# Hyena taps in pairs from both row halves, two of them ahead of the stage barrier, in a hybrid trunk kernel

## The chip, the cores and the metric

One core of one Trainium2 chip. The metric is the device time of one execution in microseconds, the median over the runs; lower is better.

## What is computed

One layer of a trunk runs over 512 latent tokens and 128 context tokens: a normalised, modulated input goes through four parallel head groups (gated DeltaNet, HGRN2, mLSTM, Hyena), their outputs are joined and projected by w_out, and a mixture of 64 experts with top 8 follows. The change touches the Hyena group's filters and, beside them, the last steps of HGRN2. Cut to what matters:

```python
def _hyena_filters(length, w1, b1, w2, b2, w3, freq):
    ...
    hid = jnp.sin(freq * (feats @ w1 + b1))
    hid = jnp.sin(freq * (hid @ w2 + b2))
    h = (hid @ w3).reshape(length, HYENA_ORDER, 2, W_D)
    ...
    h = h * jnp.exp(-tn[:, None] * deltas[None, :])[:, None, None, :]
    circ = jnp.concatenate([h[:, :, 0], zero, h[:0:-1, :, 1]], axis=0)
    circ = circ * lax.rsqrt(jnp.sum(circ * circ, axis=0, keepdims=True) + EPS)
    return jnp.fft.rfft(circ, axis=0)

def longconv(z, o):
    zf = jnp.fft.rfft(z, n=2 * l, axis=1)
    return jnp.fft.irfft(zf * hf[None, :, o], n=2 * l, axis=1)[:, :l] + dbias[o] * z

z = x1 * longconv(v, 0)
return x2 * longconv(z, 1)
```

The product hid @ w3, times the decay, gives the taps: one filter of length 512 for the latent tokens and one of length 128 for the context, five tiles of 128 lags in all.

## The kernel before, in words

All engines run programs written out by hand, with semaphores between them. SBUF is one tensor "arena", PSUM one tensor PS of eight banks of 512 f32 columns for 128 partitions. There are two stages with an all-engine barrier between them: the first (blocks from L505, TensorE's program from L619) holds the projections and the heads of the three recurrent groups, the second (from L2305, TensorE's from L2392) the Hyena group, w_out, the router, the experts and the final norm. At the seam all engines meet (end of the block, L505), meet again (L2181), GpSimd clears the stage's semaphores, and they meet a third time (L2184).

**End of the first stage.** HGRN2 goes through HU units of 128 tokens. Each has LV levels (hgrn_level, L1142 to L1154, written alternately for the two row halves of the array: partitions 0 to 63 and 64 to 127 hold two heads), whose results lie in banks 4 and 5 or 6 and 7 and are merged by DVE (L1661), then hgrn_out (L1168, L1171) in bank 2. After the last unit TensorE waits for n_on and n_taken (the last gate_heads of DVE, L1686 and L1687, which reads banks 0 and 1), transposes tiles 1 to 4 of the HGRN heads for pt 0 and 1 (L1222), and then tile 0 (L1227, behind n_last). For pt 0 the transposes go to bank 0 (tiles 1 to 3) and bank 1 (tile 4), for pt 1 to banks 4 and 5. DVE multiplies them into yT (L1737, L1738, L1742); its last step ends the stage. hid2 (the hidden layer of the filter net: 64 rows for lag tiles 0, 1, 2 and the other 64 rows for tiles 2, 3, 4) and w3sd (sum and difference of w3's sides, present in both row halves) have been in SBUF since the projections and since unit 2.

**Start of the second stage.** TensorE's order is written out at the end of its Hyena functions: filter_taps(0) to (4), forward(0, 0), forward(0, 1), filter_spectrum(0), filter_spectrum(1), prompt_spectrum, filter_norms, gate rows, and the inverse transforms. filter_taps (L2406 to L2412) makes a tile t: two matmuls (side 0 and 1) of 64 rows, 128 by 512, into banks 4 and 5 for even t and 6 and 7 for odd t; tiles 0 to 2 use rows 0 to 63, tiles 3 and 4 rows 64 to 127. A tile from the third on waits until DVE has taken the one two before it. An f32 matmul leaves two records in the trace. forward(0, j) (L2457 to L2464) is the signal's transform: 8 matmuls of 128 by 256 in banks 2j and 2j+1. filter_spectrum (L2428 to L2441) is 8 matmuls of 128 by 512 for each j (two small ones more for j = 0, L2440) in banks 4 to 7, then 0 to 3; the first waits for all five tiles (f_hs 5) and f_lag 1, the second for c_sd 2.

DVE multiplies each tile by the decay into hsd (L2723, f_hs), then takes the signal's sums and differences (L2742, L2746, L2747: c_sd), then tables(0) (L2733), a few one-row steps (L2754 to L2759: f_row), tables(1), and products (L2783 on). ACT squares each tile (L3057, f_sq) and copies the signal's odd part (L3068: c_odd) in the order: squares 0 to 3, odd part 0, square 4, odd part 1, then odd_out (L3061), table copies (L3072). POOL halves the lag-0 row of tile 0 (first_lag, L3183 and L3185: f_lag), adds the squares of tiles 1, 2, 3 to that of tile 0 (L3193: f_sum; each waits for its square, and ACT's next square waits for the sum before), then halves the row of tile 4 and makes gate_diag (L3200). SP loads the inverse's and the context's transform matrices at the start of the stage (L2310, L2311) and w_out later, behind f_H 3.

Of the kernel before, what the change touches and what calls it, by code (L numbers as in the profile page):

```python
# [17 lines left out]
P = 128  # L18
# [106 lines left out]
def trunk_program(nc, T):  # L125
# [14 lines left out]
    with ctx:  # L140
# [359 lines left out]
        filt_in, siren_step = sem("filt_in"), sem("siren_step")  # L500
        SIREN = dict(layer1=1, phase1=2, hidden1=3, layer2=4, phase2=5, hidden2=6)
# [3 lines left out]
        with nc.Block() as block:  # L505
# [113 lines left out]
            def _(pe):  # L619
# [581 lines left out]
                for u in range(HU):  # L1201
# [12 lines left out]
                    if u < NO_STATE:  # L1214
                        hgrn_state(u)
                pe.wait_ge(n_on, 3)
                pe.wait_ge(n_taken, 4)
                for pt in range(2):
                    b = 4 * pt
                    for t in range(1, NT):  # L1220
                        dst = PS[:, b, t * P:(t + 1) * P] if t < 4 else PS[:, b + 1, 0:P]
                        mm = pe.transpose(dst, o_tok[:, 1, t, P * pt:P * pt + P], ident)  # L1222
                    mm.then_inc(n_tr, 1)
# [8 lines left out]
            def _(dve):  # L1232
# [500 lines left out]
                for pt in range(2):  # L1733
                    dve.wait_ge(n_tr, 5 + pt)
                    y, b = yT[:, 2 + pt, :], 4 * pt
                    dst, src = by_column(y)[:, 16:, :], PS[:, b, P:SMP].rearrange("p (w r) -> p w r", r=SMP // GW)
                    dve.tensor_tensor(dst, dst, src, ALU.mult)  # L1737
                    dve.tensor_tensor(y[:, SMP:TOK], y[:, SMP:TOK], PS[:, b + 1, 0:P], ALU.mult)  # L1738
# [566 lines left out]
        with nc.Block() as block:  # L2305
# [86 lines left out]
            def _(pe):  # L2392
# [12 lines left out]
                def filter_taps(t):  # L2405
                    if t >= 2:  # L2406
                        pe.wait_ge(f_hs, t - 1)
                    r, a = (slice(0, HD), t * P) if t < 3 else (slice(HD, P), (t - 2) * P)
                    for side in range(2):
                        mm = pe.matmul(PS[:, 4 + 2 * (t % 2) + side, :], hid2[r, a:a + P],  # L2410
                                       w3sd[r, side].rearrange("p o n -> p (o n)"), start=True, stop=True)
                    mm.then_inc(f_h, 1)  # L2412
# [106 lines left out]
                for t in range(NT):  # L2519
                    filter_taps(t)  # L2520
                forward(0, 0)
                forward(0, 1)
                filter_spectrum(0)
# [193 lines left out]
            def _(dve):  # L2717
                dve_order = Steps(dve, "dve_order2")
                MAGIC = 12582912.0
                for t in range(NT):  # L2720
                    dve.wait_ge(f_h, t + 1)
                    b = 4 + 2 * (t % 2)
# [318 lines left out]
            def _(act):  # L3041
# [8 lines left out]

                def tap_squares(t):
                    act.wait_ge(f_hs, t + 1)
                    if t in (0, 4):
                        act.wait_ge(f_lag, t // 4 + 1)
                    if t >= 2:
                        act.wait_ge(f_sum, t - 1)
# [17 lines left out]
                for t in range(4):  # L3074
                    tap_squares(t)
# [103 lines left out]
            def _(pool):  # L3179
                pool_order = Steps(pool, "pool_order2")  # L3180
                def first_lag(t):
                    pool.wait_ge(f_hs, t + 1)
# [134 lines left out]
```

## Time and profile before

| | us |
|---|---|
| median of 3 runs | 1543.38 |
| lowest and highest run | 1539.85 and 1554.34 |
| the profiled execution's own time | 1555.77 |
| its span in the trace | 1553.9 |

The times in the rows count from the start of the span. PE is TensorE's matmuls, PEld its weight loads, DVE VectorE, ACT ScalarE, POOL GpSimd. [...] A code such as L2410 is the line of the kernel. The busy shares of the page are averages over stages with different limits; the stretch around the change is 750 to 830 us.

### The profile page before, as it was taken

The page shows a single profiled execution, that of the slowest core. Times are in us where ns is not written, and L with a number is a line of the kernel's source. Part 1 is how long each engine was busy: PE and PEld are TensorE (multiplying, and loading weights), DVE is VectorE, ACT ScalarE, POOL GpSimd, SP SyncE. Part 2 cuts the span into 40 slices and gives each one's busy share as a digit, 9 for nine tenths or more (in the row PEclk, how much of TensorE's full clock was granted, in tenths as well). Part 3 has the DMA queues.
Part 4 walks back from the last instruction along what each step waited for, and adds up shares of the span by engine and source line. Part 5 has one row for each costly group of instructions (what it writes and reads, how often), then busy time and mean ns, then how long its engine had stood idle before and what let it go on. Part 6 is the DMA issues. An engine that isn't in the chain of part 4 may idle for free. (4 is left out here: it accounts for less than half of the span.)

```text
span 1553.9 us, 21870 instructions
## 1 busy us (share of the span) xinstructions
PE 1414.2 (91%) x8304; PEld 1056.7 (68%) x8304; DVE 699.2 (45%) x1267; ACT 415.5 (27%) x810; POOL 314.9 (20%) x450
## 2 busy tenths in 40 slices
PE   5999999999899999899798897899999999999855
PEld 1678776767898888455455446678888888888611
DVE  2656876402646663677555313543222222222246
ACT  2212021314555545333122012332222222222111
POOL 0200000102111210454342220022111112111073
PEclk9999799999999999999698996999999999999989
DMA  9645411139200000000111400179999999998787
GB/s 361 204 149 186 139 55 54 55 106 421 82 1 1 1 1 23 12 9 18 44 41 68 164 8 1 73 272 386 389 380 380 378 391 394 387 392 317 239 332 285
DMA packets 101058, 279.78 MB, mean 180 GB/s; under 512 B 22609, under 2 KB 39251, under 8 KB 99580
## 3 DMA queue, kind: packets, MB, share of 16 engines
q1 hardware_dynamic: 85148, 235.55, 41.4%
q0 software_dynamic: 15840, 43.28, 7.3%
q8 instruction: 46, 0.75, 0.2%
q14 instruction: 24, 0.20, 0.0%
HBM read 230.97 MB, written 64.52 MB: 190 GB/s over the span
## 5 line engine op out<-in xcount | busy, mean ns | idle before, releaser
L2663 PEld LDWEIGHTS PS<-arena 128*128 128x128 f32 x2240 | 260.1, 193 | 42.9 <-ACT arena L3147 26.3
L2663 PE MATMUL PS<-arena 128*128 128x128 f32 x2240 | 264.4, 277 | 5.2 <-DMA arena<-in_exp_w_down 3.8
L2966 DVE TENSOR_SCALAR arena<-PS,arena 128x1024 f32<-128x1024 f32 x70 | 89.9, 1284 | 141.5 <-PE PS L2671 141.5
L2671 PE MATMUL PS<-arena 128*128 128x512 f32 x280 | 137.8, 614 | 0.8 <-DVE arena L2959 0.8
L844 PE MATMUL PS<-arena 128*128 128x320 f32 x384 | 111.4, 445 | 1.5 <-DVE arena L1257 1.5
L849 PE MATMUL PS<-arena 128*128 128x320 f32 x384 | 107.3, 432 | 0.0
L3153 ACT ACTIVATE arena<-PS 128x128 f32<-128x128 f32 x70 | 19.4, 278 | 313.8 <-PE PS L2663 313.8
L2959 DVE TENSOR_TENSOR arena<-arena,PS 128x128 f32<-128x128 f32 x70 | 20.1, 288 | 184.1 <-ACT arena L3153 184.1
L844 PEld LDWEIGHTS PS<-arena 128*128 128x128 f32 x384 | 74.4, 196 | 33.1 <-issue 5.1
L849 PEld LDWEIGHTS PS<-arena 128*128 128x128 f32 x384 | 73.0, 190 | 30.4
L857 PE MATMUL PS<-arena 128*128 128x256 f32 (+1 forms) x400 | 89.7, 383 | 0.0
L857 PEld LDWEIGHTS PS<-arena 128*128 128x128 f32 x400 | 75.4, 212 | 14.1 <-issue 6.1
L3249 POOL DMA_INDIRECT arena<-h_rows,arena x70 | 71.7, 1025 | 58.4 <-POOL arena L3246 58.4
L3147 ACT ACTIVATE arena<-PS 128x1024 f32<-128x1024 f32 x70 | 71.7, 1024 | 42.8 <-PE PS L2655 42.8
L3246 POOL COPY arena<-arena 128x1 uint32 (+1 forms) x70 | 12.8, 183 | 319.9 <-DVE arena L2957 298.0
L1316 DVE SCALAR_TENSOR_TENSOR arena<-arena 128x1024 f32<-128x1024 f32 x56 | 69.0, 1279 | 15.4 <-DMA arena<-in_w_mod 15.0
L2655 PE MATMUL PS<-cst,arena 128*128 128x128 f32 x560 | 73.0, 273 | 0.7 <-issue 0.7
L2671 PEld LDWEIGHTS PS<-arena 128*128 128x128 f32 x280 | 47.4, 189 | 37.3 <-issue 34.6
L1478 DVE TENSOR_TENSOR arena<-PS,cst 128x512 f32<-128x512 f32 x50 | 34.6, 692 | 74.8 <-PE PS L901 74.8
L2655 PEld LDWEIGHTS PS<-cst,arena 128*128 128x128 f32 x560 | 67.1, 188 | 1.5 <-issue 1.5
L2712 PE MATMUL PS<-arena,cst 128*128 128x512 f32 x80 | 41.9, 652 | 28.2 <-DMA arena<-y_rows,arena 28.2
L910 PE MATMUL PS<-arena 128*128 128x128 f32 x480 | 63.0, 284 | 0.0
(467 smaller groups left out, 2199.8 us busy)
## 6 DMA issues: line engine op xcount, KB each, us to landing
arena<-in_exp_w_gate SPq DMA_DIRECT2D x70, 512.0 KB, 6.0
arena<-in_exp_w_up SPq DMA_DIRECT2D x70, 512.0 KB, 9.1
arena<-in_exp_w_down SPq DMA_DIRECT2D x70, 512.0 KB, 16.9
y_rows<-arena SPq DMA_DIRECT2D x70, 512.0 KB, 17.0
y_rows<-cst SPq DMA_DIRECT2D x1, 21504.0 KB, 58.4
arena<-in_w_in SPq DMA_DIRECT2D x16, 1024.0 KB, 5.8
arena<-in_w_mod SPq DMA_DIRECT2D x32, 512.0 KB, 3.6
arena<-in_w_mod SPq DMA_DIRECT2D x4, 2048.0 KB, 15.1
```

Of the source, the lines that this page charges most:

```text
L844: pe.matmul(PS[:, b0, 0:TOK // 2], w[:, k, i * P:(i + 1) * P], hT[:, k, 0:TOK // 2], start=(k == 0), stop=(k == KT - 1))
L849: mm = pe.matmul(PS[:, b1, 0:TOK // 2], w[:, k, i * P:(i + 1) * P], hT[:, k, TOK // 2:TOK], start=(k == 0), stop=(k == KT - 1))
L857: mm = pe.matmul(PS[:, b0, 0:rhs.shape[2]], src[:, k, i * P:(i + 1) * P], rhs[:, k, :], start=(k == 0), stop=(k == KT - 1))
L910: mm = pe.matmul(PS[:, bank_b(x), P * h:P * h + P], gPm[x][:, h, :], gTT[x][:, h, :], start=n == 1 and h == 0, stop=h == 3, skip_group_che ...
L1316: i = dve.scalar_tensor_tensor(out=mod_acc[c], in0=mod_chunk[q % 2], scalar=scond[:, k, c:c + 1], in1=mod_acc[c], op0=ALU.mult, op1=ALU.add)
L2655: mm = pe.transpose(PS[:, k // 4, (k % 4) * P:(k % 4 + 1) * P], xg[j][:, k:D:KT], ident)
L2663: mm = pe.matmul(PS[:, bank, 0:P], w[:, k, :], xT[j % 2][:, k, :], start=k == 0, stop=k == KT - 1)
L2671: mm = pe.matmul(PS[:, 4 + 2 * (j % 2) + half, :], hid[j % 2], ed[j][:, 512 * half:512 * half + 512], start=True, stop=True)
L2712: mm = pe.matmul(PS[:, 4 + 2 * (t % 2) + half, :], ident, back[n % GB][:, 512 * half:512 * half + 512], start=k == 4, stop=k == TOPK - 1)
L2966: dve.tensor_scalar(yb[j].rearrange("p (h n) -> p h n", h=2), PS[:, 4 + 2 * (j % 2):6 + 2 * (j % 2), :], gate_col[j % 2], None, ALU.mult). ...
L3147: act.activation(xT[j % 2].rearrange("p (h k) n -> p h (k n)", h=2), PS[:, 0:2, :], ACT.Copy).then_inc(e_xT, 1)
L3249: pool.indirect_dma_start(xg[j], None, T["h2_rows"], bass.IndirectOffsetOnAxis(token_col[j], 0), bounds_check=TOK - 1, oob_is_err=False).t ...
```

## The change

A function tap_product (one matmul of a tap tile, usable in both stages) and an order of the tiles, TAP_ORDER = (0, 3, 1, 4, 2), are added. The eight tap records of tiles 0 and 3 (four matmuls, side 0 of both, then side 1 of both) are issued at the end of the first stage, behind hgrn_out of the last unit and ahead of the transposes of the HGRN heads, into banks 4 to 7; ahead of them stand waits for h_ke and siren_step. The transposes for pt 1 move from banks 4 and 5 to bank 1, and tile 4's go to columns 0 to 127 of bank 0 or 1. In the second stage TensorE begins with forward(0, 0), then tiles 1 and 4 in the same alternation, forward(0, 1), tile 2, then filter_spectrum(0) as before. DVE, ACT and POOL take the tiles in the new order (ACT's squares 0, 3, 1, 2, then odd part 0, then 4).

```diff
--- before.py
+++ after.py
@@ -498,6 +498,13 @@
         w3sd = part(r2_at + 5156, 1024).rearrange("p (s o n) -> p s o n", s=2, o=2)
         fcol, hid2 = small(3), small(HALF)
         filt_in, siren_step = sem("filt_in"), sem("siren_step")
+        TAP_ORDER = (0, 3, 1, 4, 2)
+
+        def tap_product(eng, t, side):
+
+            bank = 4 + 2 * (TAP_ORDER.index(t) % 2) + side
+            r, a = (slice(0, HD), t * P) if t < 3 else (slice(HD, P), (t - 2) * P)
+            return eng.matmul(PS[:, bank, :], hid2[r, a:a + P], w3sd[r, side].rearrange("p o n -> p (o n)"), start=True, stop=True)
         SIREN = dict(layer1=1, phase1=2, hidden1=3, layer2=4, phase2=5, hidden2=6)
         FILT1, FILT2 = 16 * 10, 16 * 13
         s_out = sem("s_out")
@@ -1213,12 +1220,16 @@
                     hgrn_out(u)
                     if u < NO_STATE:
                         hgrn_state(u)
+                pe.wait_ge(h_ke, HU)
+                pe.wait_ge(siren_step, SIREN["hidden2"])
+                for side in range(2):
+                    for t in TAP_ORDER[0:2]:
+                        tap_product(pe, t, side)
                 pe.wait_ge(n_on, 3)
                 pe.wait_ge(n_taken, 4)
                 for pt in range(2):
-                    b = 4 * pt
                     for t in range(1, NT):
-                        dst = PS[:, b, t * P:(t + 1) * P] if t < 4 else PS[:, b + 1, 0:P]
+                        dst = PS[:, pt, t % 4 * P:(t % 4 + 1) * P]
                         mm = pe.transpose(dst, o_tok[:, 1, t, P * pt:P * pt + P], ident)
                     mm.then_inc(n_tr, 1)
                 pe.wait_ge(n_last, 1)
@@ -1732,10 +1743,10 @@
                 dve.tensor_tensor(first_heads, first_heads, spread(norm_row[:, 1, :], 1, 4), ALU.mult).then_inc(n_last, 1)
                 for pt in range(2):
                     dve.wait_ge(n_tr, 5 + pt)
-                    y, b = yT[:, 2 + pt, :], 4 * pt
+                    y, b = yT[:, 2 + pt, :], pt
                     dst, src = by_column(y)[:, 16:, :], PS[:, b, P:SMP].rearrange("p (w r) -> p w r", r=SMP // GW)
                     dve.tensor_tensor(dst, dst, src, ALU.mult)
-                    dve.tensor_tensor(y[:, SMP:TOK], y[:, SMP:TOK], PS[:, b + 1, 0:P], ALU.mult)
+                    dve.tensor_tensor(y[:, SMP:TOK], y[:, SMP:TOK], PS[:, b, 0:P], ALU.mult)
                 dve.wait_ge(n_tr, 7)
                 for pt in range(2):
                     dst, src = by_column(yT[:, 2 + pt, :])[:, 0:16, :], PS[:, 3, P * pt:P * pt + P].rearrange("p (w r) -> p w r", r=SMP // GW)
@@ -2402,13 +2413,11 @@
                                        gdiag[n % 2][:, 4 * half:4 * half + 4, :].rearrange("p k n -> p (k n)"), start=True, stop=True)
                     mm.then_inc(o_gr, 1)
 
-                def filter_taps(t):
-                    if t >= 2:
-                        pe.wait_ge(f_hs, t - 1)
-                    r, a = (slice(0, HD), t * P) if t < 3 else (slice(HD, P), (t - 2) * P)
+                def filter_taps(first, tiles):
+                    pe.wait_ge(f_hs, first)
                     for side in range(2):
-                        mm = pe.matmul(PS[:, 4 + 2 * (t % 2) + side, :], hid2[r, a:a + P],
-                                       w3sd[r, side].rearrange("p o n -> p (o n)"), start=True, stop=True)
+                        for t in tiles:
+                            mm = tap_product(pe, t, side)
                     mm.then_inc(f_h, 1)
 
                 def filter_norms():
@@ -2516,10 +2525,10 @@
                                        start=False, stop=k == 7)
                     mm.then_inc(o_ps, 1)
 
-                for t in range(NT):
-                    filter_taps(t)
                 forward(0, 0)
+                filter_taps(2, TAP_ORDER[2:4])
                 forward(0, 1)
+                filter_taps(3, TAP_ORDER[4:5])
                 filter_spectrum(0)
                 filter_spectrum(1)
                 prompt_spectrum()
@@ -2717,9 +2726,10 @@
             def _(dve):
                 dve_order = Steps(dve, "dve_order2")
                 MAGIC = 12582912.0
-                for t in range(NT):
-                    dve.wait_ge(f_h, t + 1)
-                    b = 4 + 2 * (t % 2)
+                for n, t in enumerate(TAP_ORDER):
+                    if n >= 2:
+                        dve.wait_ge(f_h, n // 2)
+                    b = 4 + 2 * (n % 2)
                     i = dve.tensor_tensor(hsd[:, t], PS[:, b:b + 2, :].rearrange("p s (o n) -> p s o n", o=2),
                                           spread(spread(decay[:, t, :], 1, 2), 1, 2), ALU.mult)
                     i.then_inc(f_hs, 1)
@@ -3048,12 +3058,15 @@
                                            PS[:, GATE_BANK[n] + half, :].rearrange("p (k q) -> p k q", k=4), ACT.Copy)
                     i.then_inc(o_gt, 1)
 
+                SQUARES = (0, 3, 1, 2, 4)
+
                 def tap_squares(t):
-                    act.wait_ge(f_hs, t + 1)
+                    act.wait_ge(f_hs, TAP_ORDER.index(t) + 1)
                     if t in (0, 4):
                         act.wait_ge(f_lag, t // 4 + 1)
-                    if t >= 2:
-                        act.wait_ge(f_sum, t - 1)
+                    n = SQUARES.index(t)
+                    if n >= 2:
+                        act.wait_ge(f_sum, n - 1)
                     act.activation(hsum if t == 0 else hsq, hsd[:, t], ACT.Square).then_inc(f_sq, 1)
 
                 def odd_out(j):
@@ -3071,7 +3084,7 @@
                     act.wait_ge(f_Ht, j + 1)
                     act.activation(Htab[:, :, j, :, 2, :], Htab[:, :, j, :, 0, :], ACT.Copy).then_inc(f_h1, 1)
 
-                for t in range(4):
+                for t in SQUARES[0:4]:
                     tap_squares(t)
                 signal_odd_out(0, 0)
                 tap_squares(4)
@@ -3179,7 +3192,7 @@
             def _(pool):
                 pool_order = Steps(pool, "pool_order2")
                 def first_lag(t):
-                    pool.wait_ge(f_hs, t + 1)
+                    pool.wait_ge(f_hs, TAP_ORDER.index(t) + 1)
                     pool_order.done(pool.tensor_tensor(lag_tmp, hsd[0:1, t, 0], hsd[0:1, t, 1], ALU.add))
                     for side in range(2):
                         i = pool.tensor_scalar(hsd[0:1, t, side], lag_tmp, 0.5, None, ALU.mult)
```

## Rows read from the trace of the kernel before

**Rows 1.** The page: busy times of each engine, and the granted clock in 40 slices

```profile
PE 1414.2 (91%) x8304; PEld 1056.7 (68%) x8304; DVE 699.2 (45%) x1267; ACT 415.5 (27%) x810; POOL 314.9 (20%) x450
...
PEclk9999799999999999999698996999999999999989
```

**Rows 2.** The chain that ended last: shares by engine; pieces (start us, us, what)

```profile
PE 37%; POOL 3%; DMA 3%; issue 3%; DVE 1%; ACT 1%; SPq 0%; POOLq 0%; ACTq 0%; DVEq 0%
...
806.80 1.79 DVE arena L2733 x3
...
862.56 5.26 PE PS L2481 x16
```

**Rows 3.** Timeline of PE, 755 to 850 us: start us, us, engine, operation

```profile
759.30 1.39 PE L1222 MATMUL PS<-cst,arena 128*128 128x128 f32 x8 [2.51 <-DVE arena L1687]
...
764.66 15.67 PE L2410 MATMUL PS<-arena 64*128 64x512 f32 x20 [3.54 <-PEq L2184]
780.25 8.91 PE L2463 MATMUL PS<-arena 128*128 128x256 f32 x32
789.00 7.03 PE L2436 MATMUL PS<-arena 128*128 128x512 f32 x16
...
797.76 7.13 PE L2436 MATMUL PS<-arena 128*128 128x512 f32 x16
...
839.29 10.08 PE L2463 MATMUL PS<-arena 128*128 128x256 f32 x32 [0.56 <-ACT arena L3096]
```

**Rows 4.** Stretches: PE, PEld, DVE, ACT, POOL busy, granted clock, DMA, GB/s

```profile
756.49:759.90 3.41, 0.90 (x9) 0.79 (x9) 2.90 (x9) 0.20 (x1) 0.00 (x0) 1.00 0.00 0
...
764.60:780.25 15.65, 15.59 (x20) 5.83 (x20) 4.90 (x4) 3.06 (x3) 7.01 (x5) 0.50 0.24 84
780.25:783.70 3.45, 3.45 (x9) 2.82 (x9) 1.23 (x1) 1.06 (x1) 2.22 (x2) 0.50 0.00 0
```

**Rows 5.** Timeline of DVE's first two products; summary of PE's line L2410 (ns)

```profile
768.44 1.23 DVE L2723 TENSOR_TENSOR arena<-PS,arena 128x1024 f32<-128x1024 f32 x1 [5.92 <-PE PS L2410]
...
771.85 1.23 DVE L2723 TENSOR_TENSOR arena<-PS,arena 128x1024 f32<-128x1024 f32 x1 [2.19 <-PE PS L2410]
...
L2410 PE MATMUL PS<-arena x20: 1054/1057/1217, 764.7 to 779.3; 64*128 64x512 f32 x20
```

**Rows 6.** Stretches, one line alone (L2410, L2410, L1146): PE, PEld, clock, DMA, GB/s

```profile
768.10:771.60 3.50, 3.50 (x5) 1.33 (x4) 0.50 0.37 157
773.10:774.90 1.80, 1.80 (x5) 0.85 (x4) 0.50 0.00 0
...
747.60:748.40 0.80, 0.80 (x16) 0.80 (x16) 1.00 0.00 0
```

**Rows 7.** Timeline of DVE, POOL and ACT, 760 to 806 us

```profile
760.08 0.81 DVE L1737 TENSOR_TENSOR arena<-arena,PS 128x384 f32<-128x384 f32 x1
...
761.89 0.63 DVE L1742 TENSOR_TENSOR arena<-arena,PS 128x128 f32<-128x128 f32 x2
...
783.37 2.35 POOL L3193 TENSOR_TENSOR arena<-arena 128x1024 f32<-128x1024 f32 x1 [1.23 <-ACT arena L3057]
785.67 1.26 POOL L3183 TENSOR_TENSOR arena<-arena 1x512 f32<-1x512 f32 x1
...
790.03 1.06 ACT L3057 ACTIVATE arena<-arena 128x1024 f32<-128x1024 f32 x1 [3.69 <-POOL arena L3185]
...
791.00 0.58 ACT L3068 ACTIVATE arena<-PS 128x512 f32<-128x512 f32 x1
...
792.22 0.68 DVE L2747 TENSOR_TENSOR arena<-PS,arena 128x512 f32<-128x512 f32 x1
...
798.93 2.48 DVE L2733 TENSOR_TENSOR arena<-PS,arena 128x512 f32<-128x512 f32 x4 [6.03 <-ACT arena L3061]
...
804.93 1.02 ACT L3061 ACTIVATE arena<-PS 128x1024 f32<-128x1024 f32 x1 [2.43 <-PE PS L2436]
...
806.13 2.46 DVE L2733 TENSOR_TENSOR arena<-PS,arena 128x512 f32<-128x512 f32 x4
```

## What the change does to the time, predicted

> **What bounds the kernel now.** I read first the busy shares and the slices, then the chain of work that ended last, then PE's timeline across the stage change at 762 to 765 us, then the granted clock by stretch, then the other engines' timelines. TensorE is busy 91% of the span, and the slices show one low clock digit at slice 20, where the taps lie [rows 1]. The chain is mostly TensorE in the expert loop. Around the change it runs through DVE (Htab tables, 806.80), then POOL and DVE, and is back on PE from 862.56 on [rows 2]. So a microsecond won at 806 is won at the end, if nothing between or behind has a clock of its own. I see nothing that has: the transfers between (w_out, x again) are released by semaphores of this same stage and shift with it.
>
> PE's timeline [rows 3] has 2.51 us idle ahead of the transposes of the HGRN heads (759.30), 3.5 us idle over the barrier, then the 20 tap records (two per matmul) 764.66 to 780.25, forward 780.25 to 789.2, the filter's spectrum 0 from 789.00, spectrum 1 797.76 to 804.89. [...] The price of a tap record follows from the distance of DVE's first two products: 3.41 us for a tile of four records, 0.853 each at half clock [rows 5]; at full clock 512 columns take 0.43 (16 records in 7.13 us) [rows 3].
>
> **Do the two row halves overlap?** Before, tile 3 (rows 64 to 127) stands behind tile 2 (rows 0 to 63) once, and in 773.10 to 774.90 five records of the tap line are in flight, where 3.5 us of one half alone hold five, counting the cut ones at both ends. And HGRN's 64-row level matmuls, which alternate the halves, put 16 records into 0.80 us, 0.05 each, where 128 columns alone would need 0.43/4 = 0.11 [rows 6]. So I count two halves as fully parallel: two tiles of eight records take four slots.
> [...] The record count of group 6 speaks for the four slots.
>
> **The change in HGRN's tail.** Eight tap records are issued behind the last HGRN output (PE idle from 756.79). Four slots at 0.43 are 1.7, with 0.2 for the change of tiling 1.9 us: they end near 758.7, before the transposes can start (759.30, they wait for DVE's L1687) [rows 3]. The two waits added there (h_ke, siren_step) are long met: h_ke's last step comes before the HGRN levels that PE has just done, and the siren ran in the projection stage. Price 0. Bounds: 8 records serial at half clock are 6.8 us, to 763.6, 4.3 late; serial at full clock, or overlapped at half, 3.4 us, to 760.2, 0.9 late; below, the transposes may get the full clock and gain 0.1, no more, since DVE runs without a pause from 760.08 to its end at 762.52, which releases the barrier [rows 7]. I take 0, as the row at that place says clock 1.00 [rows 4]. Moving the transposes to banks 0 and 1 (t % 4) changes no duration and no reader: 0. Behind the inserted records stand only these transposes, and DVE waits for them alone.
>
> **The change behind the barrier.** DVE multiplies tiles 0 and 3 at once, 764.6 to 767.1 (two at 1.23) instead of waiting to 768.44. On PE: forward(0,0), 16 records of 256 columns. How soon does the clock come back? After forward's start at 780.25 it took 3.5 us; the second forward (839.29, 32 records in 10.08 us where full clock gives 6.8 and a tail of 0.2) ran some 6 us at half clock [rows 3]. I take 5.4 us, nearer to the later one since PE was idle just before, as it was there and was not before 780.25: to 770.1. That is 12.4 records at 0.43, the other 3.6 at 0.21: done 770.9. Then tiles 1 and 4, four slots: 0.2 + 1.7, 772.8. forward(0,1): 0.2 + 3.4, 776.4. Tile 2, one half only, four records at 0.43: its last starts at 777.9 and ends at 778.5. DVE's product 1.23: **T = 779.8**. Before, the last product ended at 781.6 only, but forward hid it; now spectrum 0 stands behind it with nothing between, so 1.3 us of wait are added, and still it starts at 779.9 instead of 789.00.
> The 0.2 are for the change between 64- and 128-row work. [...]
>
> **What is late next.** Spectrum 0 is 20 records, 8.8 us, done by 788.7 (790 if the clock dips again after the one-half tile and the wait). Spectrum 1 may start only when DVE has done both sums_differences (c_sd 2), which before was never late. That hangs on this row of steps behind T: ACT's square of tile 2 (1.1), POOL's third sum (2.3), POOL's first_lag(4) (785.67 to 790.03, 4.4), ACT's square of tile 4 (0.97 to the next), signal_odd_out (0.6), DVE (1.3). In the trace the third sum starts at 783.37 and DVE ends at 792.90, 9.5 us [rows 7]; with the square in front it is 10.8. So c_sd 2 falls at 779.8 + 10.8 = 790.6 (before 792.9): POOL's long sum and first_lag take the place of PE. The first two squares and sums (first_lag(0) 766 to 770.2, squares to 772.3, sum 774.8, square, sum 778.3) end before T, so they don't bind, but they are a floor: T counts as 778.3 at least.
> Then spectrum 1 starts at 790.7 instead of 797.76, 7.1 earlier; with its 7.17 us, ACT's odd_out (1.02) and 0.1 the tables(1) of DVE start at 799.0 instead of 806.13. DVE's other condition, its row work behind tables(0), takes 7.2 us from the start of tables(0) (798.93 to 806.13): 797.9, no bound [rows 7]. From tables(1) on all is as before. **Sum: 7.1 us less.**
> Its bounds: T at the floor of 778.3 gives 8.6; a clock that dips in the PE gap between the spectra (788.7 to 790.7) costs 8 records of spectrum 1 another 0.43 each, 3.4 us at most, and leaves 3.7.
>
> The profiled execution took 1555.77 us (span 1553.9 and 1.9 around it), 12.4 above the median of 1543.38. The sum is made on it, 1555.8 - 7.1 = 1548.7; the saving has nothing to do with what separates the runs (1539.85 to 1554.34), so I take it off the median: 1543.4 - 7.1 = **1536.3 us**, 0.46% less.
>
> **Rivals.**
> 1. The halves do not overlap for 512 columns. Tail 0.9 late, tiles 1 and 4 another 1.7: 7.1 - 2.6 = 4.5 less, 1538.9. For it: only one crossing of this kind in the trace. Against: both rows of group 6. 10%.
> 2. The clock stays low, and the kernel gets slower. Place: PE from 764.66 to the end of spectrum 0. For it: every tap of before ran at 0.50, and the taps now cut forward into pieces; a 1.3 us wait follows the last. Then forward 6.9, tiles 3.6, forward 7.0, tile 2 3.6, so its last record ends at 786.0 and T is 787.3; spectrum 0 takes 17.1 to 804.5 in place of 797.76, spectrum 1 7.2, and tables(1) start at 812.8: 6.7 slower, 1550.1. It decides once T passes 787: by then c_sd 2 is at 798, the break-even. Against: 3.5 us of forward alone did raise the clock [rows 4]. 5%.
> 3. A part of the saving goes to the clock: dips in the gap between the spectra or while PE waits behind the barrier, or later rises in the shifted stretch 799 to 865 where it steps between both levels. 2 to 5 less, 1540. 17%.
> 4. The clock does not fall before the barrier, since PE is busy in 756.8 to 759: then forward runs at full clock, T is at the POOL floor, 8.6 less, 1534.8. 8%.
> The forecast itself (6 to 8.5 less) 60%.
>
> **Numbers.** The runs of the same kernel spread 14.5 us, so a median of few may lie 5 us off on either side, more than most of these cases differ. From the cases (2 to 8.6 faster for more than nine in ten, around 1535 to 1541) and this spread: 1525 to 1548; rival 2 ends just outside. A measurement of this kernel tells about 1% (15.4 us) from no change. No case reaches that; only the spread can: faster 0.08, same 0.88, slower 0.04.
>
> **What would show it.** Eight tap records at 756.8 to 758.7 with the transposes still at 759.3; the barrier at the same time; DVE's product 764.6; the clock back near 770; T near 780; spectrum 0 right behind; spectrum 1 released by DVE's L2747 near 790.7, with POOL busy through 787; tables(1) 7 us earlier than 806.13. Wrong: transposes later than 759.9, T after 783, a clock of 0.50 in spectrum 0 throughout, or the saving gone by 862.56.

## The result, and the profile of the changed kernel

| | before | changed |
|---|---|---|
| median of 20 runs, us | 1543.23 | 1536.20 |
| lowest and highest, us | 1537.56 and 1556.00 | 1530.35 and 1546.50 |
| ratio, 95% interval | | 0.9943 (0.9920 to 0.9965) |
| the profiled execution, us | 1555.77 | 1546.50 |
| its span, us | 1553.9 | 1544.7 |

The change takes 7.0 us off the median; the ratio says 8.8, from 5.4 to 12.3. The forecast was 1536.3. Both profiled executions are among the slowest of their kernel, so their difference (9.3 us) is no measure of the change. Line numbers have moved: the tap product is L507 (L2410 before), forward L2472, the product of DVE L2733, the filter's spectra L2445, the second tables L2743.

PE's timeline of the changed kernel, which answers to [rows 3] (start us, us, engine, line, operation; in brackets idle time and what ended it):

```profile
756.80 3.37 PE L507 MATMUL PS<-arena 64*128 64x512 f32 x8
...
760.11 1.10 PE L1233 MATMUL PS<-cst,arena 128*128 128x128 f32 x8
...
765.40 5.38 PE L2472 MATMUL PS<-arena 128*128 128x256 f32 x16 [3.98 <-PEq L2195]
...
770.71 1.99 PE L507 MATMUL PS<-arena 64*128 64x512 f32 x8
...
776.27 1.98 PE L507 MATMUL PS<-arena 64*128 64x512 f32 x4
779.57 8.83 PE L2445 MATMUL PS<-arena 128*128 128x512 f32 x16 [1.32 <-DVE arena L2733]
788.33 1.88 PE L2449 MATMUL PS<-arena 128*1 128x512 f32 x4
790.27 7.13 PE L2445 MATMUL PS<-arena 128*128 128x512 f32 x16
```

Eight records of both halves take 1.99 us at full clock (granted clock 1.00, the whole speed; half clock is 0.50), as long as the four of one half do (1.98): four slots, as counted (a slot is the time of one record of 512 columns, 0.43 us at full clock). Spectrum 0 stands right behind DVE's last product. The stretches by granted clock, to be held against [rows 4] (PE, PEld, DVE, ACT, POOL busy, granted clock, DMA share, GB/s):

```profile
752.90:759.50 6.60, 6.38 (x23) 4.79 (x25) 2.52 (x9) 0.20 (x1) 2.21 (x1) 0.50 0.01 2
759.70:766.40 6.70, 2.72 (x19) 2.01 (x16) 3.97 (x9) 0.00 (x0) 0.00 (x0) 1.00 0.01 2
766.50:769.80 3.30, 3.30 (x9) 2.59 (x9) 1.25 (x2) 0.00 (x0) 3.01 (x3) 0.50 0.97 346
769.90:780.00 10.10, 8.78 (x33) 5.03 (x33) 3.58 (x3) 3.51 (x4) 5.80 (x3) 1.00 0.03 12
780.20:783.40 3.20, 3.20 (x5) 1.24 (x4) 1.61 (x3) 1.00 (x2) 2.72 (x2) 0.50 0.03 5
```

The clock was low over the records in HGRN's tail, high over the barrier, low for 3.3 us of forward, back at 769.9, and low once more as spectrum 0 began. The chain behind the last product, against [rows 7]:

```profile
778.29 1.23 DVE L2733 TENSOR_TENSOR arena<-PS,arena 128x1024 f32<-128x1024 f32 x1 [3.19 <-PE PS L507]
779.55 1.06 ACT L3070 ACTIVATE arena<-arena 128x1024 f32<-128x1024 f32 x1 [2.86 <-DVE arena L2733]
...
780.68 2.35 POOL L3206 TENSOR_TENSOR arena<-arena 128x1024 f32<-128x1024 f32 x1 [1.57 <-ACT arena L3070]
...
787.35 1.06 ACT L3070 ACTIVATE arena<-arena 128x1024 f32<-128x1024 f32 x1 [6.12 <-POOL arena L3198]
...
789.53 0.68 DVE L2757 TENSOR_TENSOR arena<-PS,arena 128x512 f32<-128x512 f32 x1
...
798.51 2.47 DVE L2743 TENSOR_TENSOR arena<-PS,arena 128x512 f32<-128x512 f32 x4
```

c_sd 2 comes at 790.21, 10.7 behind the last product's end (T, 779.52), and PE ends spectrum 0 within 0.1 us of it. The second tables start at 798.51 instead of 806.13: 7.6 us earlier.

The router's records start 8.2 us earlier than before (944.08 against 952.24) and take 6.2 us less. Both together would be more than the 9.3 us between the two executions. The last four matmul records of the changed kernel's profile give much of it back: they waited 5.78 us for a transfer and ran at half clock (0.50, 3.78 us), where the last four of before waited 0.50 us and took 1.98.

```profile
1530.44 3.78 PE L2721 MATMUL PS<-arena,cst 128*128 128x512 f32 x4 [5.78 <-DMA arena<-y_rows,arena]
```

### The profile page after: what moved, and what is told of

It reads as the page before. It is cut to its first block and busy times, and to the rows that moved or that the text cites. A ratio compares the mean times of both kernels' runs of the same rounds, so it can differ in the third digit from the quotient of the medians.

```text
span 1544.7 us, 21871 instructions
## 1 busy us (share of the span) xinstructions
PE 1406.5 (91%) x8304; PEld 1049.5 (68%) x8304; DVE 699.3 (45%) x1267; ACT 415.9 (27%) x810; POOL 312.9 (20%) x450
## 5 line engine op out<-in xcount | busy, mean ns | idle before, releaser
L851 PEld LDWEIGHTS PS<-arena 128*128 128x128 f32 x384 | 74.4, 196 | 33.1 <-issue 4.9
L864 PEld LDWEIGHTS PS<-arena 128*128 128x128 f32 x400 | 75.4, 212 | 14.1 <-issue 6.1
L2680 PEld LDWEIGHTS PS<-arena 128*128 128x128 f32 x280 | 47.4, 189 | 37.3 <-issue 34.6
L1489 DVE TENSOR_TENSOR arena<-PS,cst 128x512 f32<-128x512 f32 x50 | 34.6, 692 | 74.8 <-PE PS L908 74.8
```

The source lines that it names most:

```text
L851: pe.matmul(PS[:, b0, 0:TOK // 2], w[:, k, i * P:(i + 1) * P], hT[:, k, 0:TOK // 2], start=(k == 0), stop=(k == KT - 1))
L864: mm = pe.matmul(PS[:, b0, 0:rhs.shape[2]], src[:, k, i * P:(i + 1) * P], rhs[:, k, :], start=(k == 0), stop=(k == KT - 1))
L2680: mm = pe.matmul(PS[:, 4 + 2 * (j % 2) + half, :], hid[j % 2], ed[j][:, 512 * half:512 * half + 512], start=True, stop=True)
```

## The experiments

Two lengths tell most: the **stretch**, from the first record behind the barrier to the start of DVE's second tables (in forward_last, where PE waits behind the barrier, from DVE's first product), and the router's 80 records (L2587 in the changed kernel, L2578 before).

| | stretch, us | T behind the barrier | router, us | median, us | ratio to before (95%) |
|---|---|---|---|---|---|
| before | 41.5 | 16.9 | 15.3 | 1543.23 | |
| before_again | 38.0 | 15.1 | 9.1 | one run, 1544.80 | |
| the change | 33.1 | 14.1 | 9.1 | 1536.20 | 0.9943 (0.9920 to 0.9965) |
| after_again | 33.9 | 14.9 | 9.1 | one run, 1536.42 | |
| change_5 | 33.7 | 14.7 | 9.1 | 1535.95 | 0.9957 (0.9933 to 0.9980) |
| same_half | 34.6 | 15.6 | 9.1 | 1544.62 | 1.0012 (0.9988 to 1.0036) |
| behind_barrier | 38.1 | 16.4 | 9.1 | 1540.53 | 0.9999 (0.9983 to 1.0014) |
| forward_last | 36.9 | 12.6 | 15.3 | 1548.20 | 1.0040 (1.0020 to 1.0060) |
| lag_first | 33.1 | 14.1 | 9.1 | 1536.02 | 0.9983 (0.9964 to 1.0001) |
| split | 34.5 | 13.2 | 9.1 | 1537.80 | 0.9977 (0.9955 to 0.9999) |
| split_lag | 31.5 | 13.2 | 9.1 | 1539.37 | 0.9989 (0.9978 to 1.0000) |
| split_lag_2 | 31.6 | 12.4 | 9.1 | 1539.88 | 0.9987 (0.9975 to 1.0000) |
| warm_lag | 31.5 | 14.1 | 15.3 | 1540.54 | 0.9991 (0.9980 to 1.0001) |
| warm_lag_fill | 32.0 | 14.7 | 9.1 | 1532.22 | 0.9925 (0.9891 to 0.9959) |

T is the end of DVE's last tap product. The ratio is measured against runs of before in turn on the same chip and isn't the quotient of the medians. Each stretch is read from one profile. Only rows on the same chip were timed side by side: same_half, behind_barrier and forward_last; lag_first, split and split_lag; change_5, split_lag_2 and warm_lag.

**after_again and before_again.** No edit. Expected of the first:

> The changed kernel once more, for its profile alone. My theory: in every profile the stage up to DVE's second tables (L2743) is set by waits and the clock, so the barrier (first forward record) comes at 765.4 within 1 us, the last tap product (T) ends at 779.5 within 1 us, the second tables start at 798.5 within 2 us; the 5 to 6 us that the profile after shows as saved behind 945 us (router stage), where nothing was changed, come from the granted clock and are not there again to the same size. Rival: those 5 to 6 us belong to the change and stand here too, at the same place.

Measured: barrier at 763.19, 2.2 earlier than in the profile after, and T at 778.08, 1.4 earlier; both lie outside the 1 us expected. The first stage was not ahead: its transposes at 753 came 0.2 later than in after, and the steps behind them ran at full clock (1.00 from 753.3 to 757.2, where after has 0.50). The second tables at 797.06 are within the 2 us. The router took 9.12 us again, against the theory. Its 9.1 us are no accident of one execution of the changed kernel; the question goes to the kernel before.

> The kernel before once more, for its profile alone. The profile of before took 17 us at half clock over the router's matmuls (L2578, 16 us for 80 records), those of after, after_again, same_half and behind_barrier did not, forward_last did. My theory: this is a matter of how the clock's steps fall in one execution, not of the kernel, and the 5 to 6 us behind 945 us are that; so before_again either shows the router's 80 records in 9 us at a time of about 1542, or in 16 us at a time of 1550 or more. The stretch up to the second tables (L2733) stays as in before: 41 to 42 us from the first tap record to their start. Rival: before always runs the router at half clock, and the change cured that: 16 us and about 1542.

Measured: 1544.80 us with the router in 9.1. PE of before_again, and below it the same of before:

```profile
765.33 13.87 PE L2410 MATMUL PS<-arena 64*128 64x512 f32 x20 [3.35 <-PEq L2184]
779.13 7.17 PE L2463 MATMUL PS<-arena 128*128 128x256 f32 x32
...
947.87 9.12 PE L2578 MATMUL PS<-arena 128*128 128x64 f32 x80 [0.95 <-DVE arena L2865]
```

```profile
952.24 15.27 PE L2578 MATMUL PS<-arena 128*128 128x64 f32 x80 [0.95 <-DVE arena L2865]
```

The same kernel does the router in 9.1 or 15.3 us. So the 6.2 us between the router of before and that of the change are not a fixed property of the two kernels, and the rival (before always runs the router at half clock) is out. Whether the change alters how often it happens is open: one of two profiles of before has it, none of three of the change. The theory's second half does not hold: the stretch was 38.0, not 41 to 42. The clock came back inside the taps (stretches of before_again, columns as above):

```profile
773.00:776.90 3.90, 3.90 (x8) 1.52 (x6) 1.71 (x2) 2.00 (x2) 1.72 (x3) 0.50 0.00 0
777.10:779.00 1.90, 1.90 (x5) 0.67 (x4) 1.29 (x2) 0.00 (x0) 1.90 (x1) 1.00 0.00 0
```

Just ahead of 777 lie tiles 2 and 3, the one place of before where both halves work at once. But the profile of before has the same crossing at 773 to 776, and its clock stayed at 0.50 to 783.8, so the crossing alone does not explain the rise. So the stretch of before varies by 3.5 us, and the change's gain in it is 4.1 to 8.4 us, by which profiles one pairs (33.1, 33.9 and 33.7 against 41.5 and 38.0).

**same_half.**

```diff
-        TAP_ORDER = (0, 3, 1, 4, 2)
+        TAP_ORDER = (0, 1, 3, 4, 2)
-                SQUARES = (0, 3, 1, 2, 4)
+                SQUARES = (0, 1, 3, 2, 4)
```

> Tile order (0, 1, 3, 4, 2): the pairs lie in the same row half, all else as in the change. My theory (overlap of the halves): the eight records in HGRN's tail need eight slots, 3.4 us at full clock and 6.8 at half, so the transposes start at 761.0 to 763.8 in place of 760.1 and the barrier comes 1 to 3.5 us later than 765.4; the pair behind the barrier takes another 1.7 us; the second tables start at 801.5 to 804 in place of 798.5, so 2 to 5 us of the 7.6 us saved are left. Rival (only the clock and forward's place matter, the halves do not overlap at 512 columns): as the changed kernel, second tables at 798.5 within 1 us.

Measured, PE of same_half:

```profile
756.36 7.19 PE L507 MATMUL PS<-arena 64*128 64x512 f32 x8
763.49 1.97 PE L1233 MATMUL PS<-cst,arena 128*128 128x128 f32 x8
...
769.23 5.16 PE L2472 MATMUL PS<-arena 128*128 128x256 f32 x16 [3.35 <-PEq L2195]
774.32 3.70 PE L507 MATMUL PS<-arena 64*128 64x512 f32 x8
```

7.19 us in one half where both halves took 3.37, mostly at the same clock (0.50), and 3.70 where they took 1.99 (1.00 for both). The transposes wait, the barrier comes at 769.23 (3.8 later than in after, just beyond the 3.5 expected), the second tables at 803.82, and the kernel is no faster than before (0.9988 to 1.0036). The rival without overlap is out. This is also what the tail costs when it does not fit: the idle time there holds four slots, not eight.

**behind_barrier.**

```diff
-                pe.wait_ge(h_ke, HU)
-                pe.wait_ge(siren_step, SIREN["hidden2"])
-                for side in range(2):
-                    for t in TAP_ORDER[0:2]:
-                        tap_product(pe, t, side)
...
+                for side in range(2):
+                    for t in TAP_ORDER[0:2]:
+                        mm = tap_product(pe, t, side)
+                mm.then_inc(f_h, 1)
                 forward(0, 0)
...
-                    if n >= 2:
-                        dve.wait_ge(f_h, n // 2)
+                    dve.wait_ge(f_h, n // 2 + 1)
```

> The eight records of tiles 0 and 3 moved from HGRN's tail to the front of the second stage, DVE waits for them. My theory: the barrier comes 0.7 us earlier than in the change (764.7), the pair costs 3.6 us there at half clock, everything behind shifts by it less what the clock gives back, T at 781.5 to 783, second tables at 800.5 to 802, so 2 to 3.5 us of the saving are lost. Rival (the place ahead of the barrier is worth nothing, since the records there delay the barrier): second tables at 798 to 799, as in the change.

Measured: the pair took 3.79 us behind the barrier, T fell 16.4 us behind it (14.1 to 14.9 in the change), second tables 38.1. The theory's direction held, its size was short by 1 to 2 us: POOL's second sum, which starts from the first product, now ended after T (779.35 against 778.22), and in this execution the clock fell in spectrum 1 (8.68 us; 7.13 in the change). The ratio of 0.9999 (0.9983 to 1.0014) shows no saving left without the place ahead of the barrier. The clock is worth a look:

```profile
761.80:765.90 4.10, 4.07 (x9) 1.64 (x10) 0.25 (x1) 0.00 (x0) 0.00 (x0) 0.50 0.73 260
766.10:777.00 10.90, 10.86 (x44) 6.95 (x42) 4.27 (x5) 3.06 (x3) 6.55 (x4) 1.00 0.03 14
```

The clock came back at 766, behind 3.7 us of taps in both halves and 0.4 us of forward, while before 15.6 us of mostly single halves did not bring it back [rows 4]. Taps in both halves are not enough for it, as forward_last shows (3.8 us of them, the clock at 0.50 to their end and beyond).

**forward_last.**

```diff
-                forward(0, 0)
                 filter_taps(2, TAP_ORDER[2:4])
-                forward(0, 1)
                 filter_taps(3, TAP_ORDER[4:5])
+                forward(0, 0)
+                forward(0, 1)
```

> Behind the barrier tiles 1 and 4, then tile 2, then both forwards (the signal's transform behind the taps again). My theory: TensorE idles 2.4 us behind the barrier until DVE has freed the banks, the taps run at half clock (three and a half us each), the last product ends earlier (778) but forward runs only from 776, the clock comes back 3.5 us after that, spectrum 0 starts at 785 in place of 779.6 and ends past 793.5, which is then later than c_sd 2: second tables at 802 to 803.5, so some 4 us of the saving are lost. Rival (POOL's chain behind the last product alone sets the time): c_sd 2 earlier, second tables at 797 to 798.

Measured, PE of forward_last (its barrier opened at 763.19):

```profile
765.60 3.79 PE L507 MATMUL PS<-arena 64*128 64x512 f32 x8 [6.39 <-DVE arena L2733]
770.71 3.78 PE L507 MATMUL PS<-arena 64*128 64x512 f32 x4 [1.33 <-DVE arena L2733]
774.42 8.74 PE L2472 MATMUL PS<-arena 128*128 128x256 f32 x32
782.99 7.03 PE L2445 MATMUL PS<-arena 128*128 128x512 f32 x16
```

```profile
765.60:769.40 3.80, 3.78 (x8) 1.18 (x8) 0.00 (x0) 0.52 (x1) 3.10 (x3) 0.50 0.62 257
```

Two waits for DVE, taps at half clock (those in both halves too, 3.78 us busy of 3.80; the clock came back only at 777.6, 3.2 us into forward), spectrum 0 19.8 us behind the barrier (14.2 in the change), second tables 36.9: each within 0.5 us of the expectation. The last product is 1.5 to 2.3 earlier, and it helps nothing, so the rival with POOL alone is out. The time is another matter: 1548.2, slower than before (1.0020 to 1.0060) though the stretch is shorter than before's. Its router took 15.3 in the profile.

**lag_first.** This puts POOL's first_lag(4) ahead of the third sum.

```diff
                 for t in range(1, 4):
+                    if t == 3:
+                        first_lag(4)
                     pool.wait_ge(f_sq, t + 1)
...
-                first_lag(4)
                 gate_diag(0)
```

> The change, with POOL's first_lag(4) ahead of its third sum of squares. My theory: spectrum 1 is bound by two things that end within 0.1 us of each other in the profile after, c_sd 2 (POOL, ACT, DVE behind the last tap product) and TensorE's own spectrum 0 with its dip of the clock. So c_sd 2 comes 3.5 to 4 us earlier (about 7 us behind the end of the last tap product in place of 10.7), but spectrum 1 starts only as early as TensorE is free, 8.8 to 10.6 us behind that product: 0 to 1.9 us earlier than in the change, by whether the clock dips. Second tables 31 to 33 us behind the first forward record (33.1 and 33.9 in the two profiles of the change). Rival (POOL's chain alone binds): 3 us or more earlier, second tables at 29.5 to 30.5.

Measured, a part of PE, POOL and ACT:

```profile
776.13 8.83 PE L2445 MATMUL PS<-arena 128*128 128x512 f32 x16 [1.32 <-DVE arena L2733]
...
779.88 2.33 POOL L3208 TENSOR_TENSOR arena<-arena 128x1024 f32<-128x1024 f32 x1
...
782.33 1.06 ACT L3070 ACTIVATE arena<-arena 128x1024 f32<-128x1024 f32 x1 [4.55 <-POOL arena L3208]
...
786.70 7.13 PE L2445 MATMUL PS<-arena 128*128 128x512 f32 x16
```

c_sd 2 came 9.1 us behind T, not 7: the fifth square waits for the third sum (one buffer for both), which I had left out. Spectrum 1 started 10.6 behind T, when PE was free, so the stretch was 33.1 as in the change. Two bounds of the same length, as the theory said. In time it gains nothing on the change: its median is as low (1536.02), its ratio to before shows a smaller saving (0.9983), and it was not timed in turn with the change.

**split.** Tile 2 between the halves of forward(0, 1).

```diff
-                forward(0, 1)
+                forward(0, 1, (0, 1))
                 filter_taps(3, TAP_ORDER[4:5])
+                forward(0, 1, (2, 3))
```

> The change, with tile 2 between the two halves of forward(0, 1), so that its product runs beside the second half. My theory: TensorE's 1.3 us wait for the last product goes and spectrum 0 starts 1.3 us earlier, but POOL's sums are not earlier by more than 0.5 us (the third sum waits for the second), so c_sd 2 and with it the second tables come 0.3 to 0.5 us earlier. Rival (TensorE binds, POOL's chain only happens to end at the same time): second tables 1.3 us earlier or more.

Measured: spectrum 0 13.7 us behind the barrier (14.2 to 14.9 in the change), c_sd 2 24.5 (24.8 to 25.6), both earlier. Against after_again, where the clock came back at nearly the same distance from the barrier, spectrum 0 is 1.3 us earlier, as expected, and c_sd 2 is 1.1 earlier, more than the 0.5 expected. But PE now waited 2.06 us for c_sd 2, the clock fell in spectrum 1 (8.83 us), and the second tables came at 34.5, 0.6 to 1.4 later than in the change, where 0.3 to 0.5 earlier was expected.

**split_lag** (both edits), and **split_lag_2**, the same kernel timed again with change_5.

> Both edits. My theory: only together do they free spectrum 1: c_sd 2 is out of the way, spectrum 0 starts 1.3 us earlier. Second tables 1.3 to 3 us earlier than in the change by the clock (30 to 32 us behind the first forward record), time 1 to 3 us below the change, 0.5 to 0.7% below the kernel before. Rival (a third bound behind, ACT's or DVE's order): second tables no more than 0.5 us earlier.

> split_lag once more, on the same chip as change_5. Its stretch up to the second tables was 1.6 to 2.3 us shorter than the change's, but its whole time (1539.4) was above the change's 1536.2, which ran on another chip. My theory: that is the chip and the lot of the clock behind 800 us, so here it lies within 2 us of change_5. Rival: something behind the second tables costs 3 us more in it in every execution, and it is 3 us or more above change_5 again.

Measured: 31.5 and 31.6, as expected, and 1539.4 and 1539.9 us, not as expected. Timed together with change_5 (1535.95) it is 3.9 slower with a stretch 2.1 shorter, as the rival of split_lag_2 had it, so some 6 us are lost behind the second tables. PE of split_lag_2, then of change_5, at the inverse transforms and the second forward, and change_5's clock:

```profile
812.30 9.79 PE L2491 MATMUL PS<-arena 128*128 128x256 f32 x32 [5.44 <-DVE arena L2818]
...
831.00 8.83 PE L2472 MATMUL PS<-arena 128*128 128x256 f32 x32 [0.56 <-ACT arena L3111]
...
853.03 6.45 PE L2491 MATMUL PS<-arena 128*128 128x256 f32 x16 [7.18 <-DVE arena L2818]
```

```profile
804.12 5.57 PE L2412 MATMUL PS<-arena,cst 128*128 128x512 f32 x8
...
811.49 7.17 PE L2490 MATMUL PS<-arena 128*128 128x256 f32 x32 [0.94 <-DVE arena L2816]
...
827.58 7.14 PE L2472 MATMUL PS<-arena 128*128 128x256 f32 x32 [0.56 <-ACT arena L3109]
...
847.91 5.88 PE L2490 MATMUL PS<-arena 128*128 128x256 f32 x16 [7.17 <-DVE arena L2816]
```

```profile
801.20:807.80 6.60, 6.60 (x20) 4.53 (x20) 5.69 (x7) 1.24 (x3) 6.23 (x4) 0.50 0.53 202
811.40:819.00 7.60, 7.51 (x37) 6.60 (x38) 4.84 (x12) 0.42 (x1) 4.07 (x3) 1.00 0.93 346
```

In change_5 the low clock fell on gate rows (L2412) that nobody waits for yet; in both profiles of split_lag the gate rows were done at full clock (3.68 us), PE then idled 5.0 and 5.4 us, and the inverse, on the critical path, ran its first part at half clock (in split_lag_2 0.50 from 812.3 to 817.5): 2.6 us more. The second forward took another 1.7 more and the inverse at 853.03 another 0.6. Together they are 4.9 of the 5.0 us by which split_lag_2 needs longer from its second tables to the router (147.2 against 142.2). So in these two profiles the clock takes the gain away, in steps that were not edited. split_lag's profile has the same three steps long (10.05, 8.83 and 6.59 us).

**change_5.**

> The changed kernel timed again, beside the kernel before and the two below on one chip. My theory: 0.3 to 0.6% below before (5 to 9 us), second tables (L2743) 33 to 34 us behind the first forward record. Rival (the saving measured at first came in part from the lot of the clock behind 800 us): 1 to 4 us below before, though the stretch up to the second tables is as short as in the two profiles of the change.

Measured 1535.95, ratio 0.9957 (0.9933 to 0.9980), stretch 33.7: 6.6 us by the ratio. The saving is there a second time, as the theory had it.

**warm_lag.** lag_first, and one matmul whose result is not used, in PE's wait for the last product.

```diff
                 filter_taps(3, TAP_ORDER[4:5])
+                pe.wait_ge(f_hs, 4)
+                pe.matmul(PS[:, 7, :], fwd5[:, 0, 0, 0:P], fwd5.rearrange("p q t n -> p (q t n)")[:, 0:512], start=True, stop=True)
```

> The change with first_lag(4) ahead of POOL's third sum, and one more matmul of full rows (two records, 0.86 us, result not used) in TensorE's wait for the last product, so that the clock does not fall in spectrum 0. My theory: in the profiles of the change and of lag_first the clock fell for 3.4 us as spectrum 0 began and this put its end at 10.6 us behind the last product; with the clock held spectrum 1 starts 9.1 to 9.2 us behind it, bound by c_sd 2 (whose last square waits for the third sum, as the profile of lag_first shows). Second tables 31.5 to 32 us behind the first forward record, 1.5 us earlier than the change, the time 0.5 to 2.5 us below change_5 in the median. Rival (one matmul does not hold the clock): spectrum 0 again 10.6 us, second tables at 33.

Measured, PE of warm_lag and its clock at the router:

```profile
775.52 7.13 PE L2445 MATMUL PS<-arena 128*128 128x512 f32 x16 [0.26 <-DVE arena L2735]
...
784.65 7.13 PE L2445 MATMUL PS<-arena 128*128 128x512 f32 x16 [0.18 <-DVE arena L2759]
```

```profile
933.00:937.30 4.30, 3.12 (x20) 2.44 (x20) 3.92 (x5) 2.63 (x6) 0.00 (x0) 1.00 0.02 6
937.40:939.60 2.20, 2.20 (x20) 2.20 (x21) 0.00 (x0) 1.04 (x2) 0.00 (x0) 1.00 0.00 0
939.70:952.70 13.00, 13.00 (x62) 13.00 (x62) 0.00 (x0) 0.67 (x3) 0.00 (x0) 0.50 0.00 0
```

Spectrum 0 at full clock, spectrum 1 9.2 us behind T, stretch 31.5: all as expected. The time was not: 1540.5 us, 4.6 above change_5 where 0.5 to 2.5 below was expected. PE had gaps ahead of the router (3.12 busy of 4.30); the clock fell 2.2 us into it and stayed low for the rest, though PE was busy 13.00 of 13.00. The gap of 0.95 us just ahead of the router is there in all thirteen profiles without a filler, and in ten of them the router ran at full clock. What goes with the fall is when the clock had last risen: 4.6 us ahead of the router in before, forward_last and warm_lag (15.3 us), 3.5 to 4.1 us ahead in the ten others (9.1 us).

**warm_lag_fill.** One more unused matmul, in the wait ahead of the router; the wait for o_mul moves ahead of it.

```diff
                 pe.wait_ge(o_rw, 16)
+                pe.wait_ge(o_mul, 2 * NT)
+                pe.matmul(PS[:, 7, :], ident, xn[:, 0, 0:512], start=True, stop=True)
                 pe.wait_ge(n2_s, KT)
                 pe.wait_ge(n2_p, KT)
-                pe.wait_ge(o_mul, 2 * NT)
```

> warm_lag with one more unused matmul of full rows (two records) in TensorE's 0.95 us wait ahead of the router's matmuls. warm_lag had the shortest stretch to the second tables (31.5 us) and yet 1540.5 us, and its profile shows the clock at half over 62 of the router's 80 records, 15.3 us for them in place of 9.1. My theory: that fall of the clock, begun by the waits among the transposes and ahead of the router, is what takes warm_lag's gain away; with the wait filled the 80 records take 9.1 to 9.2 us and the time is 1533 to 1536. Rival 1 (one matmul does not hold the clock): 15.3 us again and 1540. Rival 2 (the router is held, but the time is lost elsewhere): 9.1 us and 1539 or more.

Measured:

```profile
937.70 1.02 PE L2583 MATMUL PS<-arena,cst 128*128 128x512 f32 x2
938.77 9.14 PE L2590 MATMUL PS<-arena 128*128 128x64 f32 x80
```

```profile
937.70:948.00 10.30, 10.25 (x85) 9.42 (x84) 0.83 (x2) 2.68 (x7) 0.00 (x0) 1.00 0.00 0
```

9.14 us, and a median of 1532.22 (nine runs, 1527.59 to 1539.85), 0.9925 of before (0.9891 to 0.9959): 8.3 us less than warm_lag for one matmul more, of which the router shows 6.2. The clock had risen 4.6 us ahead of the router, as in the three profiles where it then fell, and here it did not fall. One profile would be little, but every execution has its mean granted clock on record: 0.959 to 0.964 in all twelve of warm_lag, 0.966 to 0.971 in eight of the nine of warm_lag_fill, and 0.961 in the ninth, the longest (1539.85). In the profiles another 0.9 us is gained right behind the router, where warm_lag's low clock lasted to 956.7, and 1.6 us at 1011, where it fell once more (5.44 us against 3.81 for 32 records). It is the fastest version of the study, 4.0 below the change; it was not timed in turn with the change or with warm_lag (the chips differ), and its interval overlaps the change's. The filler was not tried alone on the change.

## Why the prediction was right

- **Overlap of the halves**: four slots for eight records, 1.99 us measured against 1.7 and 0.2. same_half, with all eight in one half, shows 3.70 at the same full clock. The four changes between 64- and 128-row work were counted at 0.2 each, the author's estimate, and after bears it out at full clock: the 16 records of forward(0, 1) between two runs of taps take 3.65 us from start to start (772.62 to 776.27), where 16 at their usual distance of 0.216 make 3.46.
- **HGRN's tail at no cost**: a size was off. The clock was 0.50 at this place in the profile after, the records took 3.37, the transposes came at 760.11 instead of 759.30 and the stage ended 0.74 later. That is the bound "overlapped at half" (0.9 late). The prediction had named transposes later than 759.9 as a sign of being wrong, and this sign came true in that profile, with little effect. From HGRN's last record to the barrier it took 8.5 us in after and 7.87 in after_again and change_5, where the records took 1.99. Without the records it took 7.87 in before and 8.2 in before_again and behind_barrier. So the term is 0 at full clock and 0.3 to 0.7 in after, at half.
- **The clock behind the barrier**: back at 769.9 where 770.1 was said. But it had also been full over the barrier, as rival 4 wanted, and fell again under forward: forward took 5.4, not 6.2. This 0.8 paid for the late barrier, so T came at 779.52 against 779.8. That the two cancelled was luck.
- **What is late next**: c_sd 2 at T + 10.7 (10.8 said), spectrum 1 at 790.27 (790.7), second tables at 798.51 (799.0). The dip of the clock in spectrum 0, mentioned in passing, made PE end at the same moment (8.83 us for its 16 records, 7.13 in warm_lag, where the clock held); lag_first, split and warm_lag show that either bound alone hides the other.
- **The sum**: 7.6 in the two profiles compared, 7.1 said, 7.0 in the medians.
- **What was wrong**: "From tables(1) on all is as before", and that nothing behind had a clock of its own. The clock's steps behind moved, in work that was not edited: the gate rows took 5.57 us in change_5, mostly at 0.50, and 3.68 in split_lag_2, at 1.00. And "the saving has nothing to do with what separates the runs": in the profile of before the router ran at half clock, which would be 6.2 us of the 12.4 by which it lay above the median, if the median execution runs it at full clock; no profile shows that. From the second tables to the router before took 146.1 and 144.6 us and the change 145.6, 142.3 and 142.2, for steps that the change does not touch. Rival 3 named shifted clock steps, but only up to 865 us, and did not see that they could also give.
- **Against before_again** the stretch saved only 4.1 to 4.8. So the chain of the prediction is shown, its agreement within 0.5 us is partly chance, and the medians (7.0 and 6.4) are what stands for the size. They hold what the clock gives or takes behind the stretch too, and how much that is has not been separated.

Open: how often each kernel runs its router at half clock, since only a profile shows the place and there are one to three of each; and what decides the course of the clock in each place.

## What to carry to other kernels

In this kernel eight tap records (64 rows, 512 columns) took 1.99 us when they alternated between the two row halves and 3.70 in one half, at full clock (after, same_half). The idle time in front of the barrier was a good place for them: where they ran at full clock (1.99 us), the barrier came 7.87 us behind HGRN's last record, as in before without them, and 0.7 us later in after, where they ran mostly at half clock (3.37 us). Look behind the stretch that you shorten, for here steps that were not edited took back the gain or more: the router's 80 records took 15.3 us in forward_last and warm_lag and 9.1 in the change, and three steps in split_lag_2 took 4.9 us more than in change_5. Where a run of narrow matmuls follows a wait, one unused matmul in the wait is worth a try: here it went with 8.3 us less (1532.22 against 1540.54), in one kernel and on another chip than the version without it. Take two profiles of a kernel before you put a difference between two profiles down to a change: here two of before differed by 11 us (1555.77 and 1544.80).

## What the runs showed of the hardware

- In three profiles (before, forward_last, warm_lag) the clock fell 2.2 us into a run of narrow matmuls (80 records of 64 columns, weights of 128) that keep PE busy without a gap, and did not come back while they lasted, 13 us (warm_lag, 13.00 busy of 13.00); in eleven it stayed full. It was full as they began in all fourteen: 15.3 or 9.1 us for the same work.
- Taps, mostly in one row half at a time, ran 15.6 us at 0.50 in before. Taps in both halves ran 3.8 us at 0.50 in forward_last and the clock stayed low behind them; in behind_barrier it was full 4.2 us after their start. PE shows as busy in all three (15.59 of 15.65 us, 3.78 of 3.80, 4.07 of 4.10), so the busy share did not tell which way the clock would go.
- The order of records in the two row halves: eight in the time of four (1.99 us at full clock in after, 3.70 for eight in one half in same_half, 1.98 for four in one half in after).
